# A transformer-like encoder layer in fp32 on one core: scan parts dealt by a list, the branch stage reordered and unrolled, feature differences moved from GpSimd to VectorE

## The reference, cut to what matters

```python
h = rmsnorm(x, g1); z = h @ W_in          # x: 2048 x 1024; z -> q | k | v | u (512) | gates (2 x 1024)
A = windowed_gqa(q, k, v)                 # window 128, ALiBi, sink
y = gelu(scan_forward(u) + scan_backward(u) + D*u)    # 32 groups of 16 channels, 64 complex states each
B = y * sigmoid(y @ W_glu + b)            # 512 x 512
merged = sigmoid(gate_a) * (A @ W_ba) + sigmoid(gate_s) * (B @ W_bs)     # 512 x 1024 each
x = x + rmsnorm(merged @ W_out)
f = gelu(dwconv3(h2 @ W_gate)) * (h2 @ W_up)          # h2 = rmsnorm(x); 1024 x 2816 each
x = x + rmsnorm(f @ W_down)
```

## Time and profile before

| | us |
|---|---|
| median of 3 runs | 2913.19 (2912.93 to 2913.23) |
| profiled execution | 2914.93 |
| its span in the trace | 2913.4 |
| PE busy in the span | 2674.1 (92%) |
| DVE, ACT, POOL busy | 1592.9, 910.8, 908.7 |
| ACT, hi half of a gate weight (L2698), mean | 1.06 |
| DVE, gate product with branch rows (L1372), mean | 0.69 |
| DVE, sum of the two branch rows (L1378), mean | 2.29 |

### The profile page before, as it was taken

One profiled execution on the slowest core, in us unless ns is written; L12 is line 12 of the kernel. 1 busy time (PEld: TensorE's weight loads), 2 busy tenths in 40 slices (PEclk: granted clock), 3 DMA queues, 4 the chain that ended last, 5 costly groups with the idle time before them and its releaser, 6 DMA issues. The chain is left out here.

```text
span 2913.4 us, 35167 instructions
## 1 busy us (share of the span) xinstructions
PE 2674.1 (92%) x12414; PEld 2190.2 (75%) x12414; DVE 1592.9 (55%) x1926; ACT 910.8 (31%) x1541; POOL 908.7 (31%) x1119
## 2 busy tenths in 40 slices
PE   6996899798999879979949999988999988999998
PEld 5885688687787667868837888866888876888886
DVE  5102674489569065444458666687667754224333
ACT  5111665531211250023333333343333323113221
POOL 2271240068784000002254344454444421001111
PEclk9998999899999989989979999999999998999999
DMA  4562232753535753444433222212222217335653
GB/s 152 144 239 74 56 73 70 210 165 116 184 105 188 134 202 123 180 166 138 152 80 122 89 87 87 80 58 80 80 87 84 83 52 234 92 91 166 171 168 108
DMA packets 360917, 361.85 MB, mean 124 GB/s; under 512 B 50000, under 2 KB 306512, under 8 KB 354768
## 3 DMA queue, kind: packets, MB, share of 16 engines
q1 hardware_dynamic: 306880, 257.03, 30.1%
q0 software_dynamic: 11440, 53.48, 5.4%
q10 hardware_dynamic: 42464, 49.60, 5.1%
HBM read 248.38 MB, written 111.67 MB: 124 GB/s over the span
## 5 line engine op out<-in xcount | busy, mean ns | idle before, releaser
L454 PE MATMUL gu_banks<-gu_b_hi,gu_a_hi 128*128 128x512 f32 x1232 | 486.4, 395 | 58.7 <-DVE gu_b_lo L812 27.7
L455 PE MATMUL gu_banks<-gu_b_hi,gu_a_lo 128*128 128x512 f32 x1232 | 484.5, 393 | 0.0
L456 PE MATMUL gu_banks<-gu_b_lo,gu_a_hi 128*128 128x512 f32 x1232 | 484.1, 393 | 0.0
L454 PEld LDWEIGHTS gu_banks<-gu_b_hi,gu_a_hi 128*128 128x128 f32 x1232 | 234.2, 190 | 115.3 <-issue 40.8
L324 PE MATMUL dn_y<-dn_w_hi,dn_f_hi 128*128 128x512 f32 x704 | 275.9, 392 | 22.1 <-DVE dn_w_lo L1164 22.1
L325 PE MATMUL dn_y<-dn_w_hi,dn_f_lo 128*128 128x512 f32 x704 | 275.1, 391 | 0.0
L326 PE MATMUL dn_y<-dn_w_lo,dn_f_hi 128*128 128x512 f32 x704 | 274.9, 390 | 0.0
L456 PEld LDWEIGHTS gu_banks<-gu_b_lo,gu_a_hi 128*128 128x128 f32 x1232 | 234.4, 190 | 49.4
L455 PEld LDWEIGHTS gu_banks<-gu_b_hi,gu_a_lo 128*128 128x128 f32 x1232 | 234.3, 190 | 48.2
L806 DVE TENSOR_TENSOR gu_a_lo<-gu_raw,gu_a_hi 128x512 fp32r<-128x512 f32 x220 | 199.6, 907 | 116.4 <-ACT gu_a_hi L738 116.4
L738 ACT ACTIVATE gu_a_hi<-gu_raw 128x512 fp32r<-128x512 f32 x220 | 138.6, 630 | 260.3 <-PE gu_banks L456 235.3
(11 more groups left out here) (288 smaller groups left out, 5512.5 us busy)
## 6 DMA issues: line engine op xcount, KB each, us to landing
dn_f_raw<-f SPq DMA_DIRECT2D x64, 704.0 KB, 5.6
gu_raw<-in_w_ffn_gate SPq DMA_DIRECT2D x44, 512.0 KB, 3.8
gu_raw<-in_w_ffn_up SPq DMA_DIRECT2D x44, 512.0 KB, 3.8
gs_w_raw<-in_w_in SPq DMA_DIRECT2D x40, 512.0 KB, 4.6
gates<-gs_gate_out ACTq DMA_DIRECT2D x64, 256.0 KB, 2.8
br_rows<-gates POOLq DMA_DIRECT2D x16, 1024.0 KB, 6.9
f<-gu_conv SPq DMA_DIRECT2D x11, 1025.0 KB, 5.2
dn_w_raw<-in_w_ffn_down POOLq DMA_DIRECT2D x22, 512.0 KB, 6.7
```

What stands on the lines that cost most here:

```text
L454: pe.matmul(out, w_hi, x_hi, start=first, stop=False, skip_group_check=again)
L455: pe.matmul(out, w_lo, x_hi, start=False, stop=False, skip_group_check=again)
L456: return pe.matmul(out, w_hi, x_lo, start=False, stop=last, skip_group_check=again)
```

## The change

- **Scan parts.** A list `scan_pace` of 40 numbers says how many parts DVE takes after each weight's split, in place of 2, 6 and 7.
- **Last store of y.** Of the eight DMAs of the last two pairs SP issues the even ones and ACT the odd ones.
- **Branches.** The order is written out: glu 0 to 3, then attn n, attn n+1, ssm n, ssm n+1 for n = 0, 2, 4, 6. All loops are unrolled. The first weights are loaded first, the first chunk of y in four pieces of 256 KB with a hi and a lo half each, the bias after them. The copies of the gated y wait only for their own four chunks and for the glu products (`chunk_free`, `product_done`). Instructions raise `chunk_free` themselves. POOL waits for the store of the block before; ACT doesn't wait between stores.
- **Feature differences.** DVE does them, in `make_operand`: after the four lo halves of j = 0 the first and third differences, after j = 1 the second, after j = 3 the fourth. POOL keeps the weight sums and multiplications.

```diff
@@ stage_gate_up, gpsimd @@
             for u in range(UNITS):
-                turning = u == PER_PASS - 1
                 if u + 1 < UNITS:
                     sum_one(u + 1)
                     sum_three(u + 1)
-                if turning:
-                    pool.wait_ge(late_in, KD * 16)
-                    for k in range(KHALF):
-                        difference_one(1, k)
-                if u + 1 < UNITS:
                     sum_two(u + 1)
...
@@ stage_gate_up, vector @@
+            def make_operand(p, j):
+                split_b(p, j)
+                for difference in {0: (difference_one, difference_three), 1: (difference_two,),
+                                   3: (difference_four,)}.get(j, ()):
+                    for k in range(KHALF):
+                        difference(p, k)
...
-                split_b(0, j)
+                make_operand(0, j)
...
@@ stage_branches @@
+        products = [("glu", b) for b in range(K)]
+        for n in range(0, n_out, 2):
+            products += [("attn", n), ("attn", n + 1), ("ssm", n), ("ssm", n + 1)]
...
+            load_weights(0)
+            for k in range(K):
+                sync.dma_start(y[:, k, columns(0)], y_rows[:, k, columns(0)]).then_inc(y_first_in[k], 16)
...
+            for n in range(n_out):
+                if n >= 2:
+                    pool.wait_ge(stored[n % 2], n // 2 * 16)
+                for h in range(2):
+                    pool.dma_start(rows[:, 2 * (n % 2) + h], gates[h, n]).then_inc(gates_in[n % 2][h], 16)
...
+            def split_weights(i):
+                if i >= len(products):
+                    return
+                s = i % 2
+                dve.wait_ge(w_raw_in[s], i // 2 * 16 + 16)
+                if i >= 2:
+                    dve.wait_ge(product_done, (i - 1) * CHUNKS)
+                dve.tensor_copy(w_hi[:, s], w_raw[:, s]).then_inc(w_hi_ready, 1)
+                dve.wait_ge(w_hi_ready, i + 1)
+                dve.tensor_tensor(w_lo[:, s], w_raw[:, s], w_hi[:, s].bitcast(F32), ALU.subtract)\
+                    .then_inc(w_lo_ready, 1)
...
+            for i, (kind, n) in enumerate(products):
+                if kind == "glu":
+                    continue
+                s, h = n % 2, 0 if kind == "attn" else 1
+                if (kind, n) == ("attn", 0):
+                    for k in range(K):
+                        keep_gated(k)
+                dve.wait_ge(gates_in[s][h], n // 2 * 16 + 16)
+                for c in range(CHUNKS):
+                    dve.wait_ge(product_done, i * CHUNKS + c + 1)
+                    dve.tensor_tensor(rows[:, 2 * s + h, columns(c)], rows[:, 2 * s + h, columns(c)],
+                                      banks[:, i % 2 * CHUNKS + c, :], ALU.mult).then_inc(chunk_free, 1)
+                split_weights(i + 2)
+                if h:
+                    dve.wait_ge(chunk_free, (i + 1) * CHUNKS)
+                    dve.tensor_tensor(rows[:, 2 * s], rows[:, 2 * s], rows[:, 2 * s + 1], ALU.add)\
+                        .then_inc(merged_ready, 1)
@@ gates_and_states @@
+    scan_pace = [1] * 4 + [4] * 12 + [2] * 4 + [7] * 4 + [16] * 2 + [5] * 7 + [6] * 3 + [4, 3, 0, 0]
...
-            for l in range(SSM_L):
+            for l in range(SSM_L) if a < QS // 2 - 1 else range(0, SSM_L, 2):
...
+        act.wait_ge(y_ready, QS)
+        last = QS // 2 - 1
+        for l in range(1, SSM_L, 2):
+            act.dma_start(y_chunks[l, :, 0:4, :], y[l * SSM_CH:(l + 1) * SSM_CH, last % 2]).then_inc(y_stored[last % 2], 16)
...
-            pair = weights[w] >= ALONE
-            for _ in range(6 + w // (N_WEIGHTS // 2) if pair else 2):
+            for _ in range(scan_pace[w]):
                 next(own_scan, None)
```

More of the change, by code:

```diff
@@ L921, in _ @@
                 if turning:
-                    split_b(1, 6)
+                    make_operand(1, 6)
 class PostNorm:
@@ L1242, in _, with load_weights @@
         def _(sync):
+            def load_weights(i):
+                if i >= 2:
+                    sync.wait_ge(w_lo_ready, i - 1)
+                kind, b = products[i]
+                weights = {"glu": w_glu, "attn": w_attn, "ssm": w_ssm}[kind]
+                sync.dma_start(w_raw[:, i % 2], weights.rearrange("(k p) n -> p k n", p=P)[:, :, b * P:(b + 1) * P])\
+                    .then_inc(w_raw_in[i % 2], 16)
+            load_weights(0)
+            for k in range(K):
+                sync.dma_start(y[:, k, columns(0)], y_rows[:, k, columns(0)]).then_inc(y_first_in[k], 16)
@@ L1251, in _ @@
+            load_weights(1)
             for k in range(K):
                 sync.dma_start(rows[:, k], attn_scratch[k * P:(k + 1) * P, :]).then_inc(rows_in[k], 16)
[L1253 to L1258 removed]
+            for i in range(2, len(products)):
+                load_weights(i)
@@ L1271, in _, with product @@
         @block.tensor
         def _(pe):
-            ws.start(pe)
-            def product(b, s, x_hi, x_lo, first=False):
-                pe.wait_ge(ws.lo_ready, b + 1)
+            def product(i):
+                kind, _ = products[i]
+                s = i % 2
+                x_hi, x_lo = (attn_hi, attn_lo) if kind == "attn" else (y_hi, y_lo)
+                pe.wait_ge(w_lo_ready, i + 1)
+                if products[i] == ("attn", 0):
+                    pe.wait_ge(attn_lo_ready, K)
+                if products[i] == ("ssm", 0):
+                    pe.wait_ge(gated_lo, K)
@@ L1288, in product @@
[L1288 to L1303 removed]
+                        if i == 0 and c == 0:
+                            pe.wait_ge(y_first_lo, k + 1)
@@ L1305, in _ @@
+                        last = split_products(pe, banks[:, s * CHUNKS + c, :], w_hi[:, s, k], w_lo[:, s, k],
+                                              x_hi[:, k, columns(c)], x_lo[:, k, columns(c)], k == 0, k == K - 1)
+                    last.then_inc(product_done, 1)
+            for i in range(len(products)):
+                product(i)
         @block.scalar
         def _(act):
-            act.wait_ge(bias_in, 16)
-            for c in range(CHUNKS):
-                cols = slice(c * BANK, (c + 1) * BANK)
-                act.wait_ge(y_in[c], 16)
-                act.activation(y_hi[:, :, cols], y[:, :, cols], ACT.Copy).then_inc(hi_ready, 1)
+            for k in range(K):
+                act.wait_ge(y_first_in[k], 16)
+                act.activation(y_hi[:, k, columns(0)], y[:, k, columns(0)], ACT.Copy).then_inc(y_first_hi, 1)
@@ L1312, in _ @@
+            for c in range(1, CHUNKS):
+                act.wait_ge(y_in[c - 1], 16)
+                act.activation(y_hi[:, :, columns(c)], y[:, :, columns(c)], ACT.Copy).then_inc(y_chunk_hi, 1)
             for k in range(K):
                 act.wait_ge(rows_in[k], 16)
-                act.activation(attn_hi[:, k], rows[:, k], ACT.Copy).then_inc(hi_ready, 1)
+                act.activation(attn_hi[:, k], rows[:, k], ACT.Copy).then_inc(attn_hi_ready, 1)
+            act.wait_ge(bias_in, 16)
             for b in range(K):
```

220 lines of the change are left out of this document (84 added, 136 removed).

## The result

The changed kernel took 2891.4 us (2890.87 to 2893.91, four runs) against 2913.2 for the kernel before on the same chip: ratio 0.9923, 95% interval 0.9912 to 0.9935. 21.8 us were gained where 31.2 had been predicted; the time lies inside the predicted range. In the profiled executions the span went from 2913.4 to 2889.5, 23.9 us.

What follows compares the result with a forecast made beforehand. TensorE sets the end in every stage touched, so only its gaps pay. Terms +1 - 1.4 - 2 - 9.2 - 8 - 12 = -31.6 took 2914.93 to 2883.3, 2881.6 as median; predicted 2882, range 2862 to 2900.

Steps and rivals of the forecast that it cites:

- rival (b): Gates: the scan's edit costs more than it brings, late load near 15, leftover stalls near 5; about +8, 2890; chance 0.15.
- the scan's edit: Gates: the new list of scan parts, gain 10.5 against price 11.5, as a whole +1 us (between -8 and +10).
- Gates' waits: Gates: four scan parts fit beside a weight's products, removing 13.0 us of waits, 2.5 of stall left; gain 10.5.
- Late load: End of the gates: POOL's load of u lands after the products, 10.5 us late, plus low clock; price 11.5.
- The 12 to 13 us of lateness: End of the gates: estimated lateness of u's load if engines take turns between queues, instead of 8.3 us.
- y store: Last store of y: issues split between SP and ACT, the last starts some 1.4 us sooner; gain 1.4.
- Branches' start: Start of the branches: first matmul about 6 us sooner, four of them turning into waits; gain 2 (0 to 3).
- Pairs: Branches: attn 1 before ssm 0 covers the 10.5 us wait, leaving a 2.6 stall; gain 9.2 (7 to 11.5).
- Differences, start: First unit of gate-and-up: VectorE's differences at 0.61 us an operation shorten the start; gain 8 (5 to 10).
- Turn: Gate-and-up, where the features are turned: VectorE's faster chain shortens TensorE's gaps; gain 12 with the clock (8 to 14).
- Rival (c): Gate-and-up: turn and start give half, another wait (POOL's sum_one for unit 23) right behind; -10, 2892; chance 0.09.

Runs made afterwards that it cites:

- late_scan: The changed kernel with two of the scan's last parts moved one wait later: 2895.0 us, ratio 0.9927.
- rev_branches: The changed kernel with the whole branches' stage of the kernel before put back: 2897.4 us, ratio 0.9944.
- whole_chunk: The changed kernel with the branches' first chunk of y as one 1 MB load, one hi copy and one lo difference: 2888.4 us, ratio 0.9907.
- split_early: The changed kernel with product 6's low half of weights made ahead of the first attention product's multiplications on VectorE: 2891.8 us, ratio 0.9917.
- four_on_dve: The changed kernel with the fourth activation sum of gate-and-up's unit 0 made by VectorE instead of GpSimd: 2895.2 us, ratio 0.9931.
- turn_order: The changed kernel with c12 and c21 of unit 21 computed ahead of operands 4 and 5 at the turn: 2891.7 us, ratio 0.992.

## Why the prediction was right, and where it was off

The direction held, and most of the mechanisms. With the gates at their measured 3.2 us the steps below add up to 24.2 us; the span fell by 23.9, and 31.6 had been forecast. That the time lies well inside the range owes something to errors that cancel: the turn and the branches' start brought 11 us less than forecast, the gates 4 more. (One slip beside the sum: rival (b), the scan's edit at +8 in place of +1, comes to 2889 and not 2890.)

- **Gates' waits, -10.5**: the products ended 10.8 us sooner after the drift of 1.1 before the stage is taken off (963.6 - 951.7 - 1.1). Right.
- **Late load, +11.5**: too dear. It cost 6.8 of wait and 2.6 at the low clock, of which 1.8 came back where 0.5 had been counted: 7.6 in all. The walk of VectorE's parts was 1.2 us too slow (the scan ended 4.6, not 3.4, ahead), and PE went on 11.4 us after the scan's end, which is the row's own figure (11.7), where I had added 2.2 for the queues beside it; this is the term that was mis-sized. The edit is worth -3.2 to -3.6, not +1. The slower load I allowed for does exist, in late_scan, where SyncE's packets start while GpSimd's are still under way; in the changed kernel nearly all of them came behind (2.5% before 956). The Trainium skill's rule ("DMA: Bandwidth & Descriptors", "Queues, rings and completion order", each engine takes turns between the queues that have work) agrees with late_scan, where the two queues had 56.4 and 47.5% of the engines. The 12 to 13 us of lateness that the prediction worked out from it did not come: 6.8 were measured.
- **y store, -1.4**: 1.4, from PE's end to SyncE's next issue (1.5 between before and rev_branches, whose branches are alike). Right.
- **Branches' start, -2**: wrong in sign, +1.9. The failed step is "the fourth chunk's low half is ready at 1038.8 as before (the bytes ahead of it are the same)". The bytes are, the loads aren't: the last low half came 21.4 us after the stage's first issue instead of 19.2, and the clock fell twice. whole_chunk, which undoes the pieces alone, has 19.4 and gives 3.5 back.
- **Pairs, -9.2**: 8.5, with the predicted stall (2.6; 3.3 measured) for the predicted reason (split_early). Right.
- **Differences, start, -8**: 8.0, but by another road: two short waits and one long one, behind a GpSimd operation of 17 us that I hadn't foreseen. It cost nothing, since VectorE's own pace bounds the unit (four_on_dve). That the size came out is partly luck.
- **Turn, -12**: 5.0, the largest miss. The direction and the chain were right, the term mis-sized. Its first gap shrank by 2.1 us as forecast (2.3); behind it I counted collisions of VectorE with GpSimd at 2 us in all and took the rest at 0.61 an operation. b_lo of the last operand alone took 5.77 us for four, b_lo of the one before 3.38, two single low halves 1.47 and 1.75: together some 6 us over their pace alone. Then 2.7 us at the low clock behind a gap that I had not counted, because it was to be small. turn_order shows that the order of c12 and c21 is not what bounds it; that VectorE's pace does is a reading of the rows.

Rival (c) gave this time (2892) for half a gain at start and turn through GpSimd's sum; the start gave all, the turn under half, and not through that sum.

## What to carry to other kernels

When the same bytes are cut into more pieces, price the arrival of what comes last, not only the first one; a head start of a few us that ends in a second wait leaves TensorE slow twice. An operation moved from GpSimd to VectorE gains its own time, but the longer unbroken run of VectorE can then hold GpSimd up or be slowed by it: count every GpSimd operation in the new stretch. Where a load's cost depends on when another queue starts behind it, look at the head start in several runs before trusting one. And look in the trace whether a wait that an experiment adds held anything up; if it didn't, the run is a repeat and no test.

## What the runs showed of the hardware

A GpSimd subtraction of 128x512 that takes 1.3 to 1.7 us stood for 17.23 while VectorE ran 27 two-input operations on the same memory back to back, and ended 1.1 us after VectorE's pause began (operations from 1495.47 to 1511.81, the end at 1512.92). It stood for 17.23 or 17.24 us in all eleven kernels in which VectorE has the differences and GpSimd this sum, and in neither of the two with the old differences; in four_on_dve the next one took 6.97, again ending 1.1 us into VectorE's next pause (1522.99 to 1524.11). The operations of VectorE took 0.61 us each all the while, as if alone.

The Trainium skill ("SBUF — State Buffer", "SBUF: two separate sides") says that the two share a port pair which the one that starts first holds for its whole instruction while the other blocks. These rows agree with the blocking, and add that GpSimd got no turn between VectorE's instructions there. Elsewhere it did. In the same trace the next sum began inside VectorE's next unbroken run:

```profile
1516.81 1.63 POOL L598 TENSOR_TENSOR gu_s_one<-gu_raw 128x512 f32<-128x512 f32 x1 [3.88 <-DMA gu_raw<-in_w_ffn_up]
1517.24 4.65 DVE L769 TENSOR_TENSOR gu_b_lo<-feat_raw,gu_b_hi 128x512 fp32r<-128x512 f32 x4
```

Here, and at the turn (5.77 for four beside GpSimd's sums of 1.6 to 1.7), it is VectorE's low halves that are slow. What decides which of the two gives way is open; no run here separates it.
